# Gate and up projections of the FFN: two of three float32r products streamed as one matmul of 512 columns

## The reference

```
h = rms_norm(x, g)                          # x * rsqrt(mean(x*x) + eps) * g
gate, up = split(h @ w_gate_up, 2)          # 1024 x 5632
x = x + (silu(gate) * up) @ w_down          # 2816 x 1024 (times 0.5 in the last four FFNs)
```

## Time and profile before

| | |
|---|---|
| Median of 3 runs | 2777.88 us (2777.1 to 2781.78) |
| The profiled execution | 2778.99 us, span 2777.2 us |
| PE busy | 2613.1 us, 94% of the span |
| DVE busy | 1834.5 us, 66% |
| ACT busy | 1266.6 us, 46% |
| Mean granted clock of TensorE | 0.973 |

### The profile page before, as it was taken

How to read it: one execution, slowest core, us unless ns; L and a number is a source line. 1 busy time by engine, 2 the same in 40 slices (tenths; PEclk the granted TensorE clock), 3 DMA queues, 4 the chain that set the end, 5 groups by cost and what they waited for, 6 DMA issues and landing times.

```text
span 2777.2 us, 51613 instructions
## 1 busy us (share of the span) xinstructions
PE 2613.1 (94%) x21578; PEld 2531.9 (91%) x21578; DVE 1834.5 (66%) x2279; ACT 1266.6 (46%) x1489; POOL 292.3 (11%) x419
## 2 busy tenths in 40 slices
PE   7998854999999999999999999999999999999998
PEld 6998744999899988998999999999999999999998
DVE  3756778655666675554656656996656656986655
ACT  3434422533456565333434334665434334665433
POOL 7000481000300010000000000140000000140000
PEclk9999877999999999999999999999999999999999
DMA  4454101455567773553554554443554554443553
GB/s 172 179 182 166 31 1 30 155 195 181 157 178 160 159 167 106 185 183 120 183 189 167 197 181 161 155 148 143 183 184 168 195 183 159 155 153 140 183 182 121
DMA packets 77780, 433.01 MB, mean 156 GB/s; under 512 B 20224, under 2 KB 22784, under 8 KB 27728
## 3 DMA queue, kind: packets, MB, share of 16 engines
q1 hardware_dynamic: 58720, 410.25, 40.7%
q0 software_dynamic: 5888, 17.53, 5.2%
q10 hardware_dynamic: 13040, 3.34, 0.6%
HBM read 426.80 MB, written 3.24 MB: 155 GB/s over the span
## 4 chain that ended last, share of the span: by engine, by line
PE 86%; DVE 8%; ACT 3%; POOL 2%; issue 1%; DMA 1%; ACTq 0%; DVEq 0%; POOLq 0%
PE psum L1854 25%; PE psum L1856 25%; PE psum L1855 25%; PE psum L2143 1%; PE psum L1953 1%; PE psum L1887 1%; DVE w_lo L1309 1%; PE psum L2119 1%; PE psum L2131 1%; ACT w_hi L850 1%; DVE arena L1479 1%; DVE arena L1484 1%; PE psum L2122 1%; PE psum L1939 0%; DVE rstd L1334 0%
## 5 line engine op out<-in xcount | busy, mean ns | idle before, releaser
L1854 PE MATMUL psum<-h_hi,w_hi 128*128 128x256 f32 x4320 | 1219.7, 282 | 34.2 <-DVE h_lo L1347 15.5
L1856 PE MATMUL psum<-h_hi,w_lo 128*128 128x256 f32 x4320 | 1210.7, 280 | 0.0
L1855 PE MATMUL psum<-h_lo,w_hi 128*128 128x256 f32 x4320 | 1210.1, 280 | 0.0
L850 ACT ACTIVATE w_hi<-raw 128x2048 fp32r<-128x2048 f32 x387 | 740.2, 1914 | 908.7 <-PE psum L1856 908.7
L1309 DVE TENSOR_TENSOR w_lo<-raw,w_hi 128x2048 fp32r<-128x2048 f32 x387 | 886.1, 2290 | 388.2 <-ACT w_hi L850 388.0
L1854 PEld LDWEIGHTS psum<-h_hi,w_hi 128*128 128x128 f32 x4320 | 814.6, 189 | 45.8 <-issue 34.6
L1855 PEld LDWEIGHTS psum<-h_lo,w_hi 128*128 128x128 f32 x4320 | 815.6, 189 | 1.2 <-issue 1.0
L1856 PEld LDWEIGHTS psum<-h_hi,w_lo 128*128 128x128 f32 x4320 | 814.8, 189 | 0.0
L1854 PE MATMUL psum<-act_hi,w_hi 128*128 128x256 f32 x1536 | 430.0, 280 | 2.2 <-DVE w_lo L1309 1.5
L1856 PE MATMUL psum<-act_hi,w_lo 128*128 128x256 f32 x1536 | 429.3, 280 | 0.0
L1855 PE MATMUL psum<-act_lo,w_hi 128*128 128x256 f32 x1536 | 429.1, 279 | 0.0
(11 more groups left out here) (311 smaller groups left out, 2692.5 us busy)
## 6 DMA issues: line engine op xcount, KB each, us to landing
raw<-in_panels SPq DMA_DIRECT2D x387, 1024.0 KB, 4.8
arena<-bias_by_distance POOLq DMA_DIRECT2D x32, 384.0 KB, 7.8
x<-in_x SPq DMA_DIRECT2D x1, 1024.0 KB, 7.8
arena<-in_dft_sq ACTq DMA_DIRECT2D x2, 512.0 KB, 6.1
arena<-in_s_b SPq DMA_DIRECT2D x1, 1024.0 KB, 15.2
arena<-in_s_c SPq DMA_DIRECT2D x1, 1024.0 KB, 16.6
arena<-s_u POOLq DMA_DIRECT2D x1, 1024.0 KB, 5.1
arena<-arena POOLq DMA_DIRECT2D x32, 32.0 KB, 1.9
```

Source lines behind the costliest of these rows:

```text
L850: a.activation(w_hi[:, s, :], raw[:, s, :], ACT.Copy).then_inc(hi_ready, 1)
L1854: t.matmul(o, w[0], xin[0], start=start, stop=False, skip_group_check=True)
L1855: t.matmul(o, w[0], xin[1], start=False, stop=False, skip_group_check=True)
L1856: return t.matmul(o, w[1], xin[0], start=False, stop=stop, skip_group_check=True)
```

## The change

`h_hi` and `h_lo` become two halves of one tile, `h_parts`. In the gate and up projections a new function `into` replaces `project`: for each tile product one matmul streams both halves, 512 columns, over `w_hi` into a whole bank (left half: `w_hi` times `h_hi`, right half: `w_hi` times `h_lo`), and a second one of 256 columns adds `w_lo` times `h_hi` into the right half. A panel now has two banks, one for each column tile. The gate takes banks 0 and 1, the up panel banks 2 and 3, and a chunk therefore all four. TensorE waits, before the projections of chunk c, until both panels of chunk c-1 have been summed.

At evacuation the halves are added: ACT copies the right halves into `fix`, a place in `arena` (`copy_fix`), and DVE adds the left halves from PSUM to them (`add_fix`, with a count in `summed`), and only then multiplies by `rstd`, in SBUF. The sum of squares of a norm before an FFN goes to bank 7 instead of 3, and bank 7 is cleared after that. `down` and all other stages keep three matmuls of 256 columns. Some semaphores are merged (`zeros_set`, `rope_squared`).

```diff
-        h_hi = sb("h_hi", [P, KT, S], F32R)
-        h_lo = sb("h_lo", [P, KT, S], F32R)
+        h_parts = sb("h_parts", [P, 2, KT, S], F32R)
+        h_hi, h_lo = h_parts[:, 0], h_parts[:, 1]
...
+        fix = arena[:, 0:4 * S].rearrange("p (m t s) -> p m t s", m=2, t=2)
...
-        SUMS_BANK = {True: 3, False: 4}
+        SUMS_BANK = {True: 7, False: 4}
+
+        def wide(m):
+            return psum[:, 2 * m:2 * m + 2, :].rearrange("p t (a s) -> p t a s", a=2)
...  ACT
+                def copy_fix(c, m, p, i=None):
+                    def at(v, per):
+                        return v if i is None else i * per + v
+                    a.wait_ge(panel_done, at(p + m + 1, 6))
+                    if i is not None or c:
+                        a.wait_ge(summed, at(2 * (f * FFC + c) + m - 1, 4))
+                    a.activation(fix[:, m], wide(m)[:, :, 1], ACT.Copy).then_inc(fix_copied, 1)
+
+                copy_fix(0, 0, n0)
                 split(n0 + 3)
                 silu(0, n0)
+                copy_fix(0, 1, n0)
                 with a.Fori(0, (FFC - 1) // 2) as i:
                     for c in (1, 2):
                         p = hidden_panel(n0, c)
                         split(p + 2, i, 6)
+                        copy_fix(c, 0, p, i)
                         split(p + 3, i, 6)
                         silu(c, p, i)
+                        copy_fix(c, 1, p, i)
                         split(p + 4, i, 6)
...  DVE
+                def add_fix(dst, c, m, i):
+                    n = 2 * (f * FFC + c) + m + 1
+                    n = n if i is None else i * 4 + n
+                    v.wait_ge(fix_copied, n)
+                    v.tensor_tensor(dst, wide(m)[:, :, 0], fix[:, m], ALU.add).then_inc(summed, 1)
+                    v.wait_ge(summed, n)
 
                 def scale_gate(c, p, i=None):
-                    v.wait_ge(panel_done, p + 1 if i is None else i * 6 + p + 1)
-                    v.tensor_tensor(gate[:, c % 2], tiles(2 * c), rstd_2, ALU.mult).then_inc(scaled, 1)
+                    add_fix(gate[:, c % 2], c, 0, i)
+                    v.tensor_tensor(gate[:, c % 2], gate[:, c % 2], rstd_2, ALU.mult).then_inc(scaled, 1)
...
-                    v.wait_ge(panel_done, at(p + 2, 6))
-                    v.tensor_tensor(act[:, b], tiles(2 * c + 1), rstd_2, ALU.mult).then_inc(scaled, 1)
+                    add_fix(act[:, b], c, 1, i)
+                    v.tensor_tensor(act[:, b], act[:, b], rstd_2, ALU.mult).then_inc(scaled, 1)
...  TensorE
+                def into(n, m, i=None, parts=None):
+                    t.wait_ge(lo_ready, n + 1 if i is None else i * 6 + n + 1)
+                    for k, j in [(k, j) for k in range(KT) for j in range(2)] if parts else \
+                            [(k, j) for j in range(2) for k in range(KT)]:
+                        if parts and j == 0 and k % 2 == 0:
+                            t.wait_ge(parts[0], parts[1] + k // 2 + 1)
+                        o, w = bank[2 * m + j], weights(n, k * COLS + j * P)
+                        t.matmul(o[:, :].rearrange("p (a s) -> p a s", a=2), w[0], h_parts[:, :, k],
+                                 start=(k == 0), stop=False, skip_group_check=True)
+                        last = t.matmul(o[:, S:2 * S], w[1], h_hi[:, k], start=False, stop=(k == KT - 1),
+                                        skip_group_check=True)
+                    last.then_inc(panel_done, 1)
...
-                project(n0, 0, parts=(h_lo_ready, 4 * st["hs"]))
-                t.wait_ge(zeros_set, 1)
-                for b in range(4):
+                into(n0, 0, parts=(h_lo_ready, 4 * st["hs"]))
+                t.wait_ge(const_set, 4)
+                for b in range(3):
+                    clear(b)
                 t.wait_ge(sq_added, 3 * (st["hn"] - st["whole"]))
                 t.matmul(bank[SUMS_BANK[True]][:, 0:S], ones[:, :], h[:, 0], start=True, stop=True).then_inc(ss_ready, 1)
-                project(n0 + 1, 1)
+                into(n0 + 1, 1)
                 t.wait_ge(rms_ready, st["hn"] + 1)
+                clear(3)
                 with t.Fori(0, (FFC - 1) // 2) as i:
                     for c in (1, 2):
                         p = hidden_panel(n0, c)
-                        t.wait_ge(act_ready, i * 2 + (f * FFC + c - 1))
-                        project(p, 2 * c, i, 6)
-                        project(p + 1, 2 * c + 1, i, 6)
+                        t.wait_ge(summed, i * 4 + 2 * (f * FFC + c))
+                        into(p, 0, i)
+                        into(p + 1, 1, i)
                         down(c - 1, p + 2, i)
```

## The result

The changed kernel takes 2807.28 us (median of 4 runs, 2806.97 to 2809.97) where the kernel before took 2777.49 beside it (2775.22 to 2781.78). The ratio is 1.011, with a 95% interval of 1.0094 to 1.0126. It is slower by 30 us. The forecast was 2760, and the range ended at 2790. The profiled execution of after took 2807.02 us with a span of 2805.2, 28.0 us more span than before.

A forecast was written before the change was run, and what follows sets the result against it. TensorE's rate of starting matmuls was taken as the bound; pairs gain 43.6 us, costs of 14.7 + 8.2 + 2.4 = 25.3 leave -18.3, so 2778.99 becomes 2760.7 profiled, stated as 2760 us, with an 8-in-10 range of 2736 to 2790.

The forecast's parts named there:

- The price of the pair: Gate and up projections: wide 0.220 plus narrow 0.1175 makes 0.3375 us against 0.353, a gain of 43.6 us.
- fp32's 0.216: Sum of squares in plain fp32: taken as 512 columns in 0.216 us, the basis for the wide matmul's 0.220.
- the float32r row of 0.230: Clearing of the banks: 512 columns at 0.230 us each, set aside for its four runs of 128; would leave 15 us gain.
- the columns decide: Rival on gate and up pairs: time goes by columns, gain only 15 us against 25 of starts, 2788 us; chance 0.28.
- The break-even: Gate and up products: a gain of 0.009 us each, a pair of 0.344 us, makes the change worth nothing.
- The starts: Between chunks 0 and 1: TensorE waits 2.1 us in seven FFNs, 14.7 in all; 9.7 in the first, 8.2 net.
- The clock: First FFN: the 9.7 us pause brings the lower granted clock once, costing 2.4 us; nothing for the seven others.
- the rival of a fall at every start: FFN starts: pauses of 2.1 us already lower the clock, seven more times 2.4 us, making 2777 us; chance 0.06.
- the pause of 1.53 us: Before the first down in the kernel before: followed by no low clock slice; expected to go with the change.
- The loop: Later chunks: the wait for summed stays covered by down, with 4.0 us of cover left, so nothing is paid.
- The rival of a wait in the loop: Later chunks: evacuation slips by more than 4.0 us, each us beyond costing 80 us over 80 chunks; chance 0.04.
- Everything small vanishes: Rival on gate and up pairs: wide 0.216 and narrow 0.114 us, gain 65 us, time 2738 us; chance 0.16.

The follow-up runs named there:

- e4: Kernel before plus unused matmuls of many types, widths and runs behind its end; whole time means nothing, float32r of 512 columns with data 0.229 us.
- e12: Changed kernel with each tile's pairs grouped, eight wide matmuls and then eight narrow; 2779.26 us, ratio to before 1.0009.
- e11: Kernel before plus unused wide and narrow matmuls behind its end, in several orders; whole time means nothing, pair mostly 0.353 us in turn, 0.345 by eights.
- e14: Changed kernel with its pairs grouped by two, two wide matmuls and then two narrow; 2774.85 us, ratio to before 0.9995.
- e2: Changed kernel with the wait for the sums split, gate panel for all but the last, up panel for the last; 2789.88 us, ratio 1.0038.
- e3: Changed kernel with the sums' wait split by panel and DVE's twelve S5 operations moved behind the first up panel's evacuation; 2785.85 us, ratio 1.0023.
- e5: Kernel before with one fp32 matmul of 32 columns more in each FFN, ahead of chunk 0's up panel; 2776.13 us, ratio 0.9997.
- e8: Kernel before plus unused groups of 24 float32r matmuls behind its end, each after one fp32 matmul of varied columns; whole time means nothing.
- e9: Kernel before plus unused groups of 18 float32r matmuls behind its end, each after single matmuls of various kinds; whole time means nothing.

## Why the prediction was wrong

**The price of the pair: the step that failed.** The prediction put the wide matmul at 0.220 us and the narrow one at 0.1175. Its sum lost 2816 x (0.3531 - 0.3375) = 44 us there, which is nearly the whole miss: 2760 + 44 = 2804, and 2807 came. Two things were wrong in it.

- 0.220 came from fp32's 0.216 with the float32r row of 0.230 explained away by its four runs of 128. e4 has 0.229 for one, two and four runs. The row nearest by type was the right one, and it was rejected on the strength of a difference of 0.01 us between two fp32 lines. One of these, L2119, reads every second element in its runs of 128 (`rearrange("p (j z) -> p z j", z=2)`), so it differs in more than the runs. (The sixteen fp32 matmuls of the earlier trace rows are eight of the program, two rows of the trace each, which leaves the 0.216 as it is.) The wide price is worth 0.009 us of the 0.0156.
- The rest is the order. Both prices came from stretches of matmuls of one width. In turn they cost 0.0081 us a pair more than in groups (after against e12); 0.0066 of it remains against the forecast, since in groups the narrow one lies below the 0.1175 that was taken. e11 shows this with nothing else running, e12 and e14 in the kernel itself. No row of before has widths in turn, so it could not be read there; it could have been held open as a cost on both sides, and at three matmuls' price for a pair the range would have reached past 2800.

**The rival "the columns decide"** named the right side, and for the wide one alone the right price, 0.230. Its 0.3475 us for the pair is what rows of one width give, and its 2788 us is 19 us short for the same reason: it too added prices of matmuls that stand among their like. Its mechanism is only part of it: the same columns cost 0.345 us a pair in groups and 0.353 in turn.

**The break-even was right.** The prediction said that a pair of 0.344 us makes the change worth nothing. e12 has 0.345 us and a ratio of 1.0009. Part of that is luck: 5.2 us of e12 come from other matmuls in the faster spacing; without them it would have come out an estimated 5 us slower.

**The starts were right.** Six pauses of 1.8 us and one of 1.6 (2.1 forecast), 9.4 us in the first FFN (9.7), the S5 operations in between, the add behind the split; e2 and e3 took these waits out and gave back 17 and 21 us, though e3 moved what e2 had left of the first FFN's to the first `down`. The chain of DVE at the last FFN's start came operation by operation as listed, with ACT's copy done before DVE came to it.

**The clock was right.** After the long pause 5.27 - 2.82 = 2.45 us were lost at the lower clock (2.4 forecast), after the short ones nothing; the rival of a fall at every start is refuted. (The slices of the earlier trace rows could not show that the pause of 1.53 us was harmless: a slice is 69 us long, and its 9 begins at 90%. The trace of before bears it out, with a granted clock of 1.00 from 99 to 102 us.)

**The loop was right.** The wait for `summed` stays under `down`; the eight waits of the wait line are the eight starts. The rival of a wait in the loop is refuted. Read from the rows, the pauses make 12.4 us for the seven and 9.4 + 2.45 - 1.5 for the first, 22.7 us (25.3 forecast). The span grew by 28.0 us; where the other 5 us lie was not followed.

**Everything small vanishes** is refuted at its 0.216 (the float32r matmul of 512 columns takes 0.229), while its 0.114 for the narrow one exists, in every second tile of e12.

## What to carry to other kernels

Before a sum is built on a row, look at what stands before and behind the row's instruction: a matmul priced among its like can cost more in turn with another width, and putting two of a width in a row gave that back here. A row of the same type outweighs one of another type, and a reason to set it aside needs a measurement of its own. When a buffer is merged, look first at the places where nothing covers its wait, and release its halves one by one.

## What the runs showed of the hardware that was not expected

- float32r matmuls of 512 columns take 0.229 us at a granted clock of 1.00 (0.233 in some blocks), where bf16 ones of 512 take 0.216, as does one of the two rows of an fp32 matmul of 256. The Trainium skill, page TensorE: Matmul & The Clock Gate, section Back-to-back issue gap, has for the isolated gap of a warm matmul the columns at 2.4 GHz plus about 2.5 ns, 216 ns for 512: the rows agree for bf16 and fp32 and differ by 13 ns for float32r.
- At the lower clock the difference is not there. In the first FFN of after, seven pairs take 101.97 - 97.50 = 4.47 us, 0.639 each, and 768 columns at 1.2 GHz are 0.640. So what float32r loses, it loses here only at the higher clock, where 768 columns at 2.4 GHz would be 0.320 and the pair takes 0.345 to 0.353.
- float32r matmuls of 256 columns have two spacings, 0.1133 and 0.1178 us, at the same granted clock, with the same data and whether DVE and ACT are busy or not. A spacing can hold through a whole FFN, 181 us in e5, and a short fp32 matmul mostly turns it over (always in e8, not always in e9). What decides it in the program stays open, and so does why widths in turn cost more. The two are linked, since the narrow matmuls in groups change their spacing from group to group (e11, e12); whether they have one cause, no run here shows.
